# Gate and up products of an expert window, split over the depth instead of over the columns

## The reference, cut to what matters

```
a = silu(h @ w_gate[e]) * (h @ w_up[e])      # h: tokens x 1024, w_gate, w_up: 1024 x 256
a = a * comb[:, e]                           # the routing weight of each token
out += a @ w_down[e]                         # 256 x 1024
```

## Time and profile before

| | us |
|---|---|
| median of 3 runs | 537.07 (534.3 to 537.37) |
| the profiled execution | 534.07 |
| its span, first to last instruction | 532.2 |
| TensorE matmul busy | 497.3 (93%) |
| VectorE busy | 183.7 (35%) |
| ScalarE busy | 148.1 (28%) |
| GpSimd busy | 153.0 (29%) |
| loaded from HBM | 160.40 MB |

### The profile page before, as it was taken

The page is one execution under the profiler, slowest core; times in us unless marked ns, Lnnn a source line. Parts: engine busy times, 40 slices in busy tenths (PEclk is TensorE's granted clock), DMA queues, the critical chain, the costliest instruction groups (busy, mean ns, idle before and its releaser), DMA issues.

```text
span 532.2 us, 14859 instructions
## 1 busy us (share of the span) xinstructions
PE 497.3 (93%) x6205; PEld 388.0 (73%) x6206; DVE 183.7 (35%) x559; ACT 148.1 (28%) x276; POOL 153.0 (29%) x195
## 2 busy tenths in 40 slices
PE   4799999999999999999999969998999899899994
PEld 3687888888888888888888746665666566566663
DVE  0631624242424252424231442332233223233333
ACT  3012222223232222313131242323322332233221
POOL 0000010101010101010100015767676676677672
PEclk9899999999999999999999999999999999999999
DMA  8997317394959563624446974979999999999982
GB/s 352 418 442 291 139 60 283 119 426 177 437 203 431 195 248 152 249 121 159 158 159 238 389 323 180 369 308 427 427 435 429 434 425 432 432 427 434 422 342 80
DMA packets 10689, 161.94 MB, mean 304 GB/s; under 512 B 1184, under 2 KB 2464, under 8 KB 3104
## 3 DMA queue, kind: packets, MB, share of 16 engines
q1 hardware_dynamic: 10656, 161.45, 73.7%
HBM read 160.40 MB, written 1.05 MB: 303 GB/s over the span
## 4 chain that ended last, share of the span: by engine, by line
PE 85%; DMA 10%; issue 2%; DVE 1%; ACT 1%; SPq 0%; DVEq 0%; ACTq 0%
PE ps L476 81%; DMA wex<-in_ex 7%; DMA wex<-in_ada 3%; PE ps L744 1%; PE ps L770 1%; PE ps L745 1%; DVE xT L1068 1%; ACT act L449 0%; ACT L452 0%; PE ps L649 0%; PE ps L662 0%; PE ps L663 0%; PE ps L664 0%; SPq L285 0%; ACT work L452 0%
## 5 line engine op out<-in xcount | busy, mean ns | idle before, releaser
L476 PE MATMUL ps<-act,wmix 128*128 128x256 f32 x864 | 194.1, 381 | 1.0 <-DVE act L850 1.0
L476 PEld LDWEIGHTS ps<-act,wmix 128*128 128x128 f32 x864 | 161.6, 190 | 24.6 <-issue 3.5
L357 POOL TENSOR_SCALAR work<-trig,work 128x256 f32<-128x256 f32 x70 | 64.9, 936 | 61.9 <-issue 52.6
L476 PE MATMUL ps<-wex,work 128*32 128x128 f32 (+1 forms) x1840 | 70.5, 300 | 11.0 <-issue 9.8
L343 POOL TENSOR_TENSOR work<-work,trig 64x256 f32<-64x256 f32 x8 | 5.7, 718 | 252.9 <-ACT work L410 151.2
L476 PE MATMUL ps<-work 32*128 32x256 f32 (+6 forms) x864 | 72.7, 374 | 0.6 <-ACT work L470 0.6
L476 PEld LDWEIGHTS ps<-wex,work 128*32 128x32 f32 x1840 | 50.1, 111 | 28.5 <-issue 13.7
L476 PEld LDWEIGHTS ps<-work 32*128 32x128 f32 (+3 forms) x864 | 47.5, 168 | 13.3 <-issue 3.3
L467 ACT ACT_TABLE_LOAD x35 | 44.9, 1283 | 1.0 <-issue 0.4
L476 PE MATMUL ps<-act,work 128*32 128x256 f32 (+1 forms) x704 | 42.6, 362 | 2.5 <-DVE work L1035 1.3
L361 POOL TENSOR_TENSOR work<-work,trig 128x512 f32<-128x512 f32 x35 | 44.6, 1275 | 0.0
(11 more groups left out here) (181 smaller groups left out, 421.8 us busy)
## 6 DMA issues: line engine op xcount, KB each, us to landing
wex<-in_ex SPq DMA_DIRECT2D x20, 3072.0 KB, 18.5
wex<-in_ada SPq DMA_DIRECT2D x12, 2048.0 KB, 11.3
wmix<-in_ex SPq DMA_DIRECT2D x8, 3072.0 KB, 20.5
wmix<-in_mix_even SPq DMA_DIRECT2D x4, 3200.0 KB, 10.5
wmix<-in_mix_odd SPq DMA_DIRECT2D x4, 3008.0 KB, 10.7
work<-in_ex SPq DMA_DIRECT2D x4, 2048.0 KB, 19.8
wmix<-in_wo SPq DMA_DIRECT2D x2, 2048.0 KB, 8.0
act<-in_ex SPq DMA_DIRECT2D x4, 1024.0 KB, 16.7
```

Of the source, the lines that this page charges most:

```text
L357: nc.gpsimd.tensor_scalar(comb_both[:, rows], slot_row[:, rows], lane_now, None, ALU.is_equal).then_inc(comb_half, 1)
L476: return nc.tensor.matmul(out, lhsT, rhs, start=start, stop=stop, **kw)
```

## The change

The four column groups no longer share out the 512 columns. Each takes two of the eight depth tiles (2q and 2q+1) over all 512 columns, so that each band of 32 partitions in bank 0 holds a partial sum of the whole result: 8 products of 512 columns for a window instead of 32 products of 128. VectorE copies 128x512 instead of 128x128. The one transpose is replaced by four products, one for each block of 128 columns of `gu_sb`: the copied block is the stationary operand (128x128), and a new constant `stack`, four 32x32 identities on top of each other, streams with 32 columns; this transposes the block and adds its four bands. The transposed rows move from bank 0, which is now full, to the second half of bank 3. `gu_sb` (now 512 columns) lies over routing buffers that are done with by then.

```diff
@@ CONST_WIDTHS @@
+                ("stack", WIN), ...
@@ buffers @@
-        gu_sb = piece(P)
...
+        gu_sb = work[:, work_at[0]:work_at[0] + 2 * FF]
@@ turn_rows @@
-                nc.tensor.transpose(ps[:, 0, P:2 * P], rows_sb[:, 0:P], ident)
-                nc.tensor.transpose(ps[:, 0, 2 * P:3 * P], rows_sb[:, P:T], ident).then_inc(rows_turned, 1)
+                nc.tensor.transpose(ps[:, 3, T:T + P], rows_sb[:, 0:P], ident)
+                nc.tensor.transpose(ps[:, 3, T + P:2 * T], rows_sb[:, P:T], ident).then_inc(rows_turned, 1)
@@ window @@
-                for k in range(KT):
+                for i in range(2):
                     for q in range(4):
-                        last = mm(ps[q * WIN:(q + 1) * WIN, 0, 0:P], xw[:, k, :], place_gu(place, k)[:, q * P:(q + 1) * P], k == 0, k == KT - 1)
+                        last = mm(ps[q * WIN:(q + 1) * WIN, 0, :], xw[:, 2 * q + i, :], place_gu(place, 2 * q + i), i == 0, i == 1)
                 last.then_inc(gu_ready, 1)
                 gather(n + 1)
 
                 pe.wait_ge(gu_copied, n + 1)
-                nc.tensor.transpose(ps[:, 1, 0:P], gu_sb, ident).then_inc(gu_turned, 1)
+                for c in range(4):
+                    last = mm(ps[:, 1, c * WIN:(c + 1) * WIN], gu_sb[:, c * P:(c + 1) * P], co("stack"), True, True)
+                last.then_inc(gu_turned, 1)
@@ VectorE @@
-            xw_ps = ps[:, 0, P:3 * P].rearrange("p (h q n) -> p q h n", h=2, q=4)
+            xw_ps = ps[:, 3, T:2 * T].rearrange("p (h q n) -> p q h n", h=2, q=4)
...
-                v.tensor_copy(gu_sb, ps[:, 0, 0:P]).then_inc(gu_copied, 1)
+                v.tensor_copy(gu_sb, ps[:, 0, :]).then_inc(gu_copied, 1)
@@ constants @@
+    put("stack", np.concatenate([np.eye(WIN, dtype=np.float32)] * 4))
```

More of the change, by code:

```diff
@@ L36 @@
 CONST_WIDTHS = (("ident", P), ("before", P), ("swap", P), ("slot_no", WIN), ("lane_no", 1), ("mask", T),
-                ("group_no", GROUPS), ("expert_no", EXPERTS), ("less_magic", EXPERTS), ("fold", 37), ("inv_freq", 1), ("row_no", 1))
+                ("stack", WIN), ("group_no", GROUPS), ("expert_no", EXPERTS), ("less_magic", EXPERTS), ("fold", 37), ("inv_freq", 1), ("row_no", 1))
 def places(widths):
```

## The result

The change makes the kernel slower: 561.38 us median (559.4 to 562.53) against 535.68 (533.97 to 537.37) in the same comparison, ratio 1.049 with a 95% interval of 1.046 to 1.053. The forecast was 560 us, range 553 to 568. The profiled execution took 561.38 us, span 559.6.

What follows compares the result with a forecast made beforehand. TensorE bounds by a hair, with expert loads right behind. A window gains 0.04, pays 0 for the copy and 0.76 for the turn: +0.72, times 35 is 25.2, less 1.0: +24 us, median 560 us, range 553 to 568.

Steps and rivals of the forecast that it cites:

- The bound: Windows before the change: TensorE bounds by a hair, loads right behind; slower windows cost in full, faster earn next to nothing.
- The product: Gate/up product on TensorE: paid by columns, 1.70 to 1.74 us against 1.77, gain taken as 0.04 us a window.
- The copy: VectorE's copy of gate/up: 512 columns take about 0.69 us, 0.40 longer, hidden behind the gather, cost 0.
- its cover: The gather on TensorE, which hides VectorE's copy; forecast as used up to the last 0.01 us.
- The rival with the copy as the wait since before: TensorE's turn follows VectorE's copy at a fixed distance: 0.35 us a window more, +36, 572 us; chance 7%.
- The turn: Four float32 products replace TensorE's transpose: eight weight loads instead of one, +0.70 to +0.78 us a window, taken as 0.76.
- The row of products with 36 columns: Profile row of 128x128-stationary products: 15 steps of 0.111 us, paid by weight loads; used to price the transpose's replacement.
- The rival with unpipelined loads: At TensorE's transpose replacement, the eight weight loads do not overlap their matmuls: 1.4 us a window, +48, 585 us; chance 3%.
- The sum: Per window -0.04 + 0 + 0.76 = +0.72 us; 35 windows give 25.2, less 1.0 for the load: +24 us.
- the third rival: TensorE's "issue" waits, mostly at window heads, hide up to 6 us of the slowdown: +18, 554 us; chance 12%.
- the wait for a load: TensorE's one wait for an expert load, at window 496.35: expected to go, taking 1.0 us off the total.
- The low end of its own range: Main forecast's lower end, 556: 0.70 for the transpose's replacement, product gain 0.07, runs at the low end (534 + 22).

Runs made afterwards that it cites:

- the half product: The kernel before with every second depth tile of the gate/up product left out (32 matmuls of 128 columns instead of 64): 530.67 us, ratio 0.993.
- The wide product alone: The changed kernel with its 512-column gate/up product, but the 128-column copy and single transpose of the kernel before: 534.06 us, ratio 1.000.
- the four units: The changed kernel with the kernel before's narrow product and 128-column copy, keeping four float32 stack products in place of the transpose: 587.56 us, ratio 1.099.

## Why the prediction was right

- **The bound.** TensorE by a hair, the loads behind it: shown by the half product, 4 of 30 us. The wide product alone agrees, with 0 of 1 us.
- **The product.** Forecast 0.04 us less, measured 0.03 (1.77 to 1.74 us). The Trainium skill's overhead of about 60 cycles for each matmul ("TensorEngine Tiling (Array Packing)", Instruction Overhead) does not add to these rounds: 48 matmuls fewer save 0.03 us, not the estimated 1.2.
- **The copy.** 0.69 us as forecast; its cover ended within 0.01 us of where the sum had it, and both sides of that edge were measured. The rival with the copy as the wait since before is out. How little room was left shows in the run with 0.34 us more of copy, which cost some 11 us.
- **The turn.** Forecast +0.76, measured +0.75 us: 1.01 against 0.26. The row of products with 36 columns was the right one to price it by. The steps of 0.11 us between weight loads of 128 columns agree with the Trainium skill ("TensorE: Matmul & The Clock Gate", LDWEIGHTS), by which a load lasts as many 1.2 GHz cycles as it has columns, 0.107 us here; it is the distance between the loads that agrees, the trace shows one of them alone as 0.14 us long. The rival with unpipelined loads (1.4 us) is out.
- **The sum.** +0.72 forecast for a window; 0.73 in the window shown (5.74 to 6.47), 24.7 us over 34 windows and 0.75 in the last. The medians lie 25.7 us apart, the forecast was 24. The hidden part of the third rival did not appear: the head of the window idles 0.22 us for "issue" as before.
- **What it had wrong.** It took off 1.0 us for the wait for a load. The wait is gone from the list, but the same 1.0 us is idle at the same place, so this term was 0; it is more than half of the difference between 24 and 25.7. The low end of its own range, 534 + 22, leaves this term out, by which it would be 555.
- **Not foreseen** was a side effect that this change happens to avoid: it makes TensorE's loop body shorter (1119 records of TensorE's instructions in a round instead of 1693), where one that only added units paid 26 to 28 us more.

## What to carry to other kernels

When work is split over column groups, columns times rounds stays the same however it is dealt out; count what the new layout needs afterwards, and where few columns stream, as here, count it in weight loads (0.11 us for each). A wait that the profile gives to another engine may be the end of the work before it: compare the distance with a place where that engine alone is waited for. Before making a busy engine faster, read when the last load lands.

## What the runs showed of the hardware that I had not expected

TensorE's step back in a long loop has an edge in the length of the body. With 1693 records of TensorE's instructions in a round it costs 1.4 us of idle time. With 1791 (the four units, in the windows) it costs 7.6 to 7.8 us, with 1784 (the kernel before with 22 products at the end) 6.4 to 7.1. The first product after it then runs at half the clock, 3.64 us for its 64 matmuls instead of 1.95. The stretch with that product, in the run with the four units (length, busy times by engine, clock, DMA share, GB/s):

```profile
384.00:394.00 10.00, 5.16 (x80) 3.77 (x80) 0.29 (x1) 0.00 (x0) 0.38 (x1) 0.51 0.92 387
```

The page's line of the instruction queue has 27 packets for the whole execution of the kernel before, 24 for the changed kernel with 22 products, and 55 for each of the two runs with a long body. The DMA view of 375 to 500 us, a stretch of two rounds and more, shows when they come (queue: packets, MB, share). The kernel before, where the instruction queue q8 is not in the list, so that it moved nothing:

```profile
q1 hardware_dynamic: 2891, 53.75, 100.5%
q14 instruction: 1, 0.01, 0.0%
```

The four units alone:

```profile
q1 hardware_dynamic: 2550, 48.78, 93.4%
q8 instruction: 20, 0.33, 1.0%
```

The kernel before with 22 products, then the changed kernel with them:

```profile
q8 instruction: 21, 0.34, 1.0%
```

```profile
q8 instruction: 1, 0.02, 0.0%
```

So with a long body instructions are fetched all through the loop, and with the shorter one they are not fetched again. That these are TensorE's is inferred, from its list being the one that grew. Not tried were where between 1693 and 1784 the edge lies and whether it is one of records or of bytes. It is open, too, how much of the idle time is the queue behind the expert loads, which fill 93% of the DMA engines' time in that stretch.
